# Loads of state and kept weights ahead, the first block by halves, router products behind two residuals, and no spread scatter

## The reference

```python
mod = silu(cond) @ w_ada[l] + b_ada[l]             # shift, scale, gate; twice
hn = rmsnorm(x, norm_mix) * (1 + sc1) + sh1
proj = hn @ w_in[l]                                # 1024 x 3840, into 12 column blocks
# differential attention, bidirectional retention (state 64x64 per head),
# bidirectional HGRN2 (gates from sigmoid), each rms-normed per head and gated
x = x + g1 * (concat(o_da, o_ret, o_hg) @ w_out[l])
hn = rmsnorm(x, norm_ffn) * (1 + sc2) + sh2
# router shared by all layers: best of 4 groups by its top two, then top 2 of 4 experts
x = x + g2 * sum over experts e of gate[e] * (silu(hn @ w_gate[e]) * (hn @ w_up[e])) @ w_down[e]
```

## Time and profile before

| | |
|---|---|
| median of two timed executions | 916.56 us (915.92 to 917.2) |
| profiled execution, its own time | 919.49 us |
| its span | 917.6 us |
| TensorE (PE) busy | 872.9 us, 95% |
| VectorE (DVE) busy | 454.6 us, 50% |
| ScalarE (ACT) busy | 171.0 us, 19% |
| GpSimd (POOL) busy | 79.4 us, 9% |
| moved by DMA | 307.37 MB, mean 335 GB/s |

### The profile page before, as it was taken

How to read it: one execution, slowest core, us unless ns; L and a number is a source line. 1 busy time by engine, 2 the same in 40 slices (tenths; PEclk the granted TensorE clock), 3 DMA queues, 4 the chain that set the end, 5 groups by cost and what they waited for, 6 DMA issues and landing times.

```text
span 917.6 us, 13378 instructions
## 1 busy us (share of the span) xinstructions
PE 872.9 (95%) x4762; PEld 446.0 (49%) x4766; DVE 454.6 (50%) x845; ACT 171.0 (19%) x444; POOL 79.4 (9%) x110
## 2 busy tenths in 40 slices
PE   4899999989899999999999999999989999999997
PEld 1655566558743333333337455756874333333332
DVE  2395887753563323322236987876356332333222
ACT  2202015231411111110121201442231111110011
POOL 1113130000010000000011223000001000000001
PEclk9999999999999999999999999999999999999999
DMA  8997565768789999999997555474558999999993
GB/s 361 412 397 312 229 233 228 312 237 352 286 315 424 422 423 423 422 424 424 424 413 308 216 223 198 190 286 196 235 219 331 422 424 422 424 423 422 423 425 138
DMA packets 50317, 307.37 MB, mean 335 GB/s; under 512 B 8682, under 2 KB 8698, under 8 KB 16848
## 3 DMA queue, kind: packets, MB, share of 16 engines
q1 hardware_dynamic: 42368, 291.52, 78.0%
q0 software_dynamic: 4848, 12.39, 3.6%
q10 hardware_dynamic: 3040, 2.62, 0.9%
HBM read 305.45 MB, written 4.73 MB: 338 GB/s over the span
## 4 chain that ended last, share of the span: by engine, by line
PE 75%; DMA 15%; DVE 5%; ACT 2%; issue 1%; SPq 1%; DVEq 0%; ACTq 0%
PE ps L484 71%; DMA ring<-in_w_experts 10%; PE ps L519 3%; DMA wT<-in_w_in 3%; DMA ring<-in_w_ada 2%; ACT eP L1755 1%; DVE hnT L1221 1%; PE ps L551 1%; ACT hnT L1827 1%; DVE rt L1167 1%; SPq L397 0%; DVE eP L1477 0%; DVE eP L1475 0%; DVE x L1738 0%; DVE proj L1340 0%
## 5 line engine op out<-in xcount | busy, mean ns | idle before, releaser
L484 PE MATMUL ps<-ring,proj 128*64 128x512 f32 x1024 | 285.1, 596 | 1.8 <-ACT proj L2017 1.7
L484 PE MATMUL ps<-ring,hnT 128*128 128x512 f32 (+1 forms) x576 | 204.2, 505 | 4.3 <-DVE t L1566 2.3
L484 PEld LDWEIGHTS ps<-ring,proj 128*64 128x64 f32 x1024 | 86.8, 137 | 137.8 <-issue 136.2
L484 PEld LDWEIGHTS ps<-ring,hnT 128*128 128x128 f32 x576 | 106.5, 191 | 78.2 <-issue 70.3
L1722 DVE COPY proj<-ps 128x512 f32<-128x512 f32 x16 | 11.1, 692 | 122.9 <-PE ps L484 122.9
L484 PE MATMUL ps<-home_qc,proj 128*64 128x512 f32 x128 | 57.8, 594 | 3.2 <-DMA ring<-in_w_experts 3.2
L484 PE MATMUL ps<-ring,silT 128*32 128x512 f32 x384 | 46.8, 608 | 14.1 <-DMA ring<-in_w_ada 7.1
L484 PE MATMUL ps<-home_kd,proj 128*64 128x512 f32 x128 | 57.6, 593 | 0.0
L484 PE MATMUL ps<-home_ra,proj 128*64 128x512 f32 x128 | 57.6, 592 | 0.0
L1708 DVE RECIPROCAL proj<-proj 128x512 f32<-128x512 f32 x16 | 53.7, 3353 | 0.6
L1707 DVE TENSOR_SCALAR proj<-proj 128x512 f32<-128x512 f32 x16 | 6.8, 427 | 84.9 <-ACT proj L1755 84.9
(11 more groups left out here) (288 smaller groups left out, 1073.5 us busy)
## 6 DMA issues: line engine op xcount, KB each, us to landing
ring<-in_w_experts SPq DMA_DIRECT2D x128, 1024.0 KB, 17.6
ring<-in_w_ada SPq DMA_DIRECT2D x48, 1024.0 KB, 9.4
ring<-in_w_in SPq DMA_DIRECT2D x24, 1024.0 KB, 8.2
home_qc<-in_w_experts SPq DMA_DIRECT2D x16, 1024.0 KB, 15.8
home_ra<-in_w_experts SPq DMA_DIRECT2D x16, 1024.0 KB, 19.7
home_kd<-in_w_experts SPq DMA_DIRECT2D x16, 1024.0 KB, 21.2
ring<-in_w_out SPq DMA_DIRECT2D x8, 1024.0 KB, 10.8
eP<-in_w_experts SPq DMA_DIRECT2D x4, 1024.0 KB, 10.4
```

The lines of the kernel that those rows point to most:

```text
L484: ins = nc.tensor.matmul(*a, **k)
```

## The change

Eight edits, in the order of the program.

1. Block f of layer 0 is multiplied by halves of the inner dimension: all that needs the first half (`eP`), for both banks, stands before all that needs the second (`wT`). Each bank is opened by a matmul of zeros. `ADA_BEHIND` of layer 0 becomes (0, 2, 3, 3, 4, 4, 4, 4): no adaLN step behind f, two behind q, and more behind i and r.
2. ScalarE copies block b before it copies the gate rows.
3. Group 0 of block s is copied by ScalarE instead of VectorE.
4. HGRN's end state moves from behind the second normalisation to behind block s, into bank 4, with its copy and its store.
5. The three VectorE operations that scale the router's weights stand behind two of the first residuals.
6. Four zero matmuls are added between the two groups' row transposes, three before the picks are removed.
7. The kept loads of kc and es go out before the last four ring loads of the first turn. `SPREAD_FROM` is `TURNS`, so no turn spreads its scatter.
8. At the end GpSimd adds both halves of group 0, VectorE both halves of group 1.

```diff
-ADA_BEHIND = ((2, 3, 3, 3, 3, 2, 4, 4), (0, 0, 3, 3, 3, 2, 0, 0))
+ADA_BEHIND = ((0, 2, 3, 3, 4, 4, 4, 4), (0, 0, 3, 3, 3, 2, 0, 0))
...
-SPREAD_FROM = TURNS // 2
+SPREAD_FROM = TURNS
...
                 first_loads(("ro", 1), slots=(HOME["ra"], HOME["kd"]))
+                keep("kc", ("hstate",), ("rstate",))
+                keep("es", ("mixed", 0), ("mixed", 1), ("stored",), ("stored_state",))
                 first_loads(slots=TURN_ORDER[l][7:9])
                 keep("xy", ("x1", 1))
                 first_loads(slots=TURN_ORDER[l][9:])
-                keep("kc", ("hstate",))
                 keep("hn", ("rows", 1, 1))
-                keep("es", ("mixed", 0), ("mixed", 1), ("stored",), ("stored_state",))
...
+                def by_half(name, b):
+                    ss, banks = [], [b]
+                    for half in range(2):
+                        ss.append(slot(RING + half))
+                        for p in range(2):
+                            if p and not half:
+                                banks.append(next_bank())
+                            if not half:
+                                mm(ps[:, banks[p], :], zeros[:, 0:P], zeros[:, 0:BLK], start=True, stop=False, skip_group_check=True)
+                            for g in range(NG):
+                                if not p:
+                                    wait_for_input(g, half)
+                                for hl in range(2):
+                                    h = 2 * p + hl
+                                    for k in range(KH * half, KH * (half + 1)):
+                                        for d in range(2):
...
+                            if half:
+                                last.then_inc(c.fills(banks[p], "projP", name, p), 1)
...
                 modulation_by_feature(l, 1, next(turn_of_banks))
+                end_state(1, "h", T_GI, 4)
                 da_weights(1, 1)
...
                 normalized_group("hn2", "xn2", 1)
-                end_state(1, "h", T_GI)
...
                 for h in range(2):
                     row_bank(0, h, 2 - h)
+                for b in range(4, 8):
+                    mm(ps[:, b, :], zeros[:, 0:P], zeros[:, 0:BLK], start=False, stop=False, skip_group_check=True)
                 copied_group("hn2", 1)
...
                 pe.wait_ge(S("bank2_free"), c.claim(2))
-                stream_zeros(2, 3)
...
-                evac_block("s")
                 da_norm(1, 0)
...
-                st(tt(router_scaled, wrt, modT[:, 3, :, 1:2].broadcast_to([P, KC, NE]), ALU.mult), "router_scaled")
-                st(tt(router_shifts, wrt, modT[:, 2, :, 1:2].broadcast_to([P, KC, NE]), ALU.mult))
-                st(red(router_sums, router_shifts.rearrange("p k e -> p e k")), "router_sums")
...
-                for n in range(4):
+                for n in range(2):
+                    first_residual(n, 0)
+                st(tt(router_scaled, wrt, modT[:, 3, :, 1:2].broadcast_to([P, KC, NE]), ALU.mult), "router_scaled")
+                st(tt(router_shifts, wrt, modT[:, 2, :, 1:2].broadcast_to([P, KC, NE]), ALU.mult))
+                st(red(router_sums, router_shifts.rearrange("p k e -> p e k")), "router_sums")
+                for n in range(2, 4):
                     first_residual(n, 0)
...
+                        if g and l + 1 == L:
+                            half = slice(h * BLK, (h + 1) * BLK)
+                            st(tt(x[:, g, half], x[:, g, half], to, ALU.add), "x2", h)
...
                 evac_block("a")
+                evac_block("b")
                 gate_rows(l)
-                evac_block("b")
...
-                squares_of(4, 16, "dao", 1, 0)
+                squares_begun(4, "dao", 1, 0)
+                evac_block("s", 0)
+                squares_ended(4, 16, "dao", 1, 0)
+                end_state(1, "h")
...
                 swish("rg", "s", T_RG, (0,))
+                store_state(1, "o_hg", "stored_state")
...
-                end_state(1, "h")
                 shifted("hn2", 1, (0, 1))
...
-                store_state(1, "o_hg", "stored_state")
...
+                if l + 1 == L:
+                    for h, product in enumerate((first_product[0], nsq[:])):
+                        half = slice(h * BLK, (h + 1) * BLK)
+                        pool.wait_ge(c.of("x2p", 0, h), c.at("x2p", 0, h))
+                        put(g_.tensor_tensor(x[:, 0, half], x[:, 0, half], product, ALU.add), "x2a", h)
+                    return
```

More of the change, by code:

```diff
@@ L846, in _ @@
                     stream_zeros(b, 5)
[L847 to L849 removed]
+                    by_half("f", b)
+                else:
+                    ss = open_block("f")
+                    by_head_and_group("f", 0, ss, b)
+                    by_head("f", 1, ss)
                 ada_behind("f")
@@ L1728, in _ @@
                     dve.wait_ge(S(f"gate2_{g}"), c.value(f"gate2_{g}", f"A{l}", 0))
-                    for h, to in enumerate((first_product[g], nsq[:])):
+                    for h, to in enumerate((first_product[g], act if g and l + 1 == L else nsq[:])):
                         sums = f"round_sums{2 * g + h}"
```

25 lines of the change are left out of this document (15 added, 10 removed).

## The result

The changed kernel took **906.26 us** (median of 2 runs, 906.24 to 906.28) against 916.56 before: ratio 0.9888, 95% interval 0.9845 to 0.993 (the intervals below are of the same kind). It is faster by 10.3 us, not by the forecast 16.3, and 0.26 us outside the range. Its profiled execution took 906.24, span 904.4, against 919.49 and 917.6. With more runs of both kernels on two other chips, the ratio was 0.9881 (0.9863 to 0.9899) and 0.9888 (0.9868 to 0.9907).

The account below looks back on a forecast made before the run. TensorE's work and waits were taken to bound the kernel outside the expert turns, the stream of loads inside them. Terms 1.5 + 3.5 + 2.1 + 4.2 + 4.6 + 0.4 = 16.3 us gave 900.3 us, range 895.5 to 906.0.

Parts of the forecast that it names:

- block s: Block s, both layers: ScalarE's copy and the end state fill TensorE's waits, 0.9 us each, plus 1.7 of clock; 3.5 us.
- the tail: Kernel's end: VectorE's last addition, running without GpSimd's beside it, gets shorter; 0.4 us, between 0 and 0.8.
- the start: Layer 0's first block by halves starts earlier at full clock, less a wait for VectorE's queries; 1.5 us.
- loads and spread: Expert turns: earlier kc and es loads give 1.7 us in layer 0, 2.5 in layer 1; unspread scatter 0.4; 4.6 us.
- the bound for a falling clock: Layer 0's start: lower bound of the gain if the clock falls anyway, -0.2 us.
- The residual: Router products behind two first residuals: the multiply freeing TensorE's bank starts earlier; 1.05 us per layer, 2.1 in all.
- router to seats: Router to gather: earlier row shifts and removed zero matmuls gain 3.2 us in layer 0, 1.0 in layer 1.
- The 1.7 us of clock in layer 1: Layer 1, behind block s's two waits: granted clock 0.79 over 8 us, counted as gained once the gap is filled.
- the last rival: Expert turns: bunched waits lower the clock, up to 27.2 us lost, 927.5 us; chance 0.03.
- Loads and spread, 4.6 us: nearly right as a number (2.8 + 2.5 in the profile), wrong in its cause.** The false step is "the stream, which never empties from here": From the loop's first load, transfers stay full; without es the stream is 2.47 us shorter, starts 0.75 later: 1.7 us.
- Spread off is worth nothing in layer 0: Layer 0's turns 4 to 7: 0.35 us less work each gains nothing, since TensorE then waits for the stream's loads.
- The second rival: Start and block s clock terms (1.7 us each) fail, or router gains halve (2.1 less); 905.8 us, chance 0.14.

Follow-up runs that it names:

- the tenth experiment: The changed kernel with the first block and layer 0's order of adaLN steps as before the change; 908.12 us, ratio 0.9908.
- the third: The changed kernel with the kept loads kc and es back at their old places, behind the last ring loads; 908.57 us, ratio 0.9897.
- the fourteenth experiment: The changed kernel with ScalarE's k and v store issues behind the second weights' copy and VectorE's four last products before its additions; 906.16 us, ratio 0.9873.
- the fifth: The changed kernel, unchanged, run again with more timed runs; median 907.45 us, ratio 0.9881.
- the thirteenth: The changed kernel with ScalarE's issues of the k and v stores moved behind its copy of the second weights; 906.32 us, ratio 0.9875.
- the first experiment: The changed kernel with five zeroing matmuls added ahead of the wait for layer 1's picks; 907.37 us, ratio 0.9886.
- the eleventh: The first experiment's kernel with VectorE's four last products all ahead of the second group's two additions; 905.56 us, ratio 0.9873.
- experiment 8: The changed kernel with kc and es loaded late and HGRN's end state, copy and store back at the router; 914.12 us, ratio 0.9968.

## Why the prediction was right or wrong

The forecast was 16.3 us, and 10.3 were measured. Of the 6.0 us between them 2.9 are the last step, which took a sum from one profiled execution off the median of two runs. The other 3.1 are terms: block s gave 1.65 less than forecast, the low clock at layer 1's gather cost 1.6 that no term had, the tail gave 0.4 less and the start 0.1 less, and loads and spread gave 0.7 more.

**The start, 1.5 us: right**, 1.4 in the profile and 1.6 by the tenth experiment. First matmul at 31.17 (forecast 31.5), a wait of 1.60 us at the first scores (forecast up to 1.8), clock 1.00 behind it. Some luck is in the 1.5: two zeroing matmuls at the rate of three in 0.65 are 0.4 us and not 0.2, and 66.6 less 64.9 is a wait of 1.7 and not 1.8. About 1.0 of it comes only where the clock stays up, and the bound for a falling clock, -0.2, was too low: 0.55.

**The residual, 1.05 a layer, and router to seats, 3.2 and 1.0: right** to 0.05 us, three of them read from one row each. The 3.2 holds for an execution in which the clock stays up there. From the residual to layer 0's gather TensorE took 37.9 to 38.9 us in the three profiles of the old order, 34.7 in four with the new one (the changed kernel's among them), but 35.4 in six and 37.1 in two, whose clock fell.

**Block s, 3.5 us: wrong in "ScalarE's store issues fit into its idle time".** It gave 0.1 in layer 0 and 1.75 in layer 1. The prediction let TensorE wait for VectorE alone. In its place the runs show ScalarE: its copy of the weights, for which TensorE now waits, stood behind the end state's copy (0.37 us) and two issues (0.38 and 0.45). Putting only the issues behind the weights gives 0.47 and 0.36 back, and so does taking the end state out. The 1.7 us of clock in layer 1 was mis-sized as well. The kernel before had this row, where the changed one has 3.70 us:

```profile
629.56 4.78 PE L484 MATMUL ps<-ring,hnT 128*128 128x512 f32 x8
```

From its start 24 matmuls took 7.86 us instead of 8.95, that is 1.1, since for a part of the 8 us TensorE idled. And the low clock was there in only one of the three profiles of this form of the block.

**The clock gained in one place was lost in another.** TensorE now has waits of 1.12 and 0.19 us ahead of layer 1's gather, and the clock fell behind them: -1.6 us, no term of mine. This is the last rival's mechanism at another place. That rival took 2.4 us of waiting to be needed, from one row. Here the clock fell behind a wait of 1.12 us, and in block s of layer 1 of the kernel before, in one of three profiles, behind waits of 0.75 and 0.95 (ahead of the rows at 626.64 and 628.25). In the turns the page's rule (the Trainium skill, "TensorE: Matmul & The Clock Gate", "HAM oscillation — how this bites in real kernels": bursts of matmuls between waits for transfers fall to half rate again and again) did not show: with 0.96 us of waiting in one, the clock was 1.00. At the gather the first profile agrees with it, though the wait is one for VectorE. But of five profiles with this wait of 1.1 us and the clock still up ahead of it, the gather took 5.46 us in three (the changed kernel's, the third and the fourteenth experiment's) and 3.83 in two (the fifth and the thirteenth). And the filled wait of the first experiment did not help the eleventh, which has it too and fell at 670 and 700. What decides there stays open.

**Loads and spread, 4.6 us: nearly right as a number (2.8 + 2.5 in the profile), wrong in its cause.** The false step is "the stream, which never empties from here". It does empty behind the gather, to 0.54, and did so before, to 0.53. Undoing both edits costs 0.4 to 1.7 us, and leaves the loop's first load where it was. In the kernel before es held that load, since it waited for the end state's store. ScalarE's rows, of the kernel before and of the changed one:

```profile
250.94 2.16 ACTq L1805 DMA_DIRECT2D out_o_hg<-home_es  x2
```

```profile
186.66 1.38 ACTq L1838 DMA_DIRECT2D out_o_hg<-home_es  x2
```

I had seen this hold in layer 1, and booked it under moving the load. With the state stored early the first load comes 3.9 us behind the first gate product wherever es stands. But how much of the 2.8 and 2.5 us this explains is not settled. With the state late again (experiment 8) layer 1's turns lose 0.85 us and layer 0's none, 221.14 us to the layer's change beside 221.12 in the changed kernel and 223.97 before. There es happened to leave in time. No run puts the late store back into the kernel by itself so that es is late in both layers. "Spread off is worth nothing in layer 0" and the two or three late waits held.

**The tail, 0.4: nothing**. The last addition ran alone and took 0.69 us, as expected, but the one before it took 1.46 beside GpSimd's second, where the kernel before had 1.01. The prediction had priced only the last one.

**Profiles against medians.** I subtracted a sum built on one execution with three low clocks (at 33, 240 and 626) from a median of two runs, which was 0.5 to 1.7 us under the medians of the larger sets. The profile of the changed kernel had one low clock. So of the 13.2 us between the profiles some 2.5 belong to these two executions; between the kernels there are 10.3 to 10.8. The second rival, at 905.8 and with a chance of 0.14, lies within 0.5 us of the result, for the most part by luck. Gaps that shrink but do not vanish did occur. But of its two clock terms the first came (low in four of four profiles with the old start, in two of thirteen with the new), the second was smaller than it had it, and its halved router gain did not occur; a fall at the gather stood in for them.

## What to carry to other kernels

Before a load is moved ahead, ask what will use the transfers in the place that it leaves: if they wait for slots there, the move gains next to nothing. Look also at what the load itself waits for (here a store from the same room): in the kernel before this held the loads behind it. An operation moved into a gap belongs to two queues: read also what it stands ahead of on the engine that copies its result. Do not price a low clock from one profile: count in how many executions it is there, and price the work done in it, not the stretch. And take a sum that was read from a profile off that profile's own time.

## What the hardware showed beside this

TensorE's granted clock falls at a few places of this program, each in a part of the executions, and in none of the 17 profiles in the turns behind the first of a layer. Counted over the profiles: with the old start (4 profiles) it was low between 30 and 40 in all four, with the new one in 2 of 13. At layer 0's router it was low in all 3 profiles with the old order of the router's stage and in 11 of 14 with the new one; between 670 and 715 in 1 of 3 and in 12 of 14. One fall at layer 1's gather cost 1.63 us. Zeroing matmuls in the wait or among the router's products did not take the falls away: with both, in one profile, they came at 245 and 700. Whether filling one place moves the fall to another is not shown. Two additions of 128x512 on two engines at once took 1.26 (GpSimd) and 1.46 us (VectorE), against 0.69 for VectorE's alone. GpSimd's other addition took 1.26 too, beside a product that VectorE read from PSUM in its usual 0.69.
